# Attention with the keys on the partitions: maxima from a rough pass, no transposed weights

## What is computed

```
s = einsum('bkgqd,bskd->bkgqs', q, k) * scale
p = softmax(s, axis=-1)
o = einsum('bkgqs,bskd->bkgqd', p, v)
```

## Time and profile before

| | us |
|---|---|
| median of 3 runs | 1509.86 (1509.58 to 1510.22) |
| the profiled execution | 1512.08 |
| its span, first to last instruction | 1510.1 |
| TensorE busy | 1382.5 (92%) |
| VectorE busy | 920.6 (61%) |
| ScalarE busy | 597.4 (40%) |
| GpSimd busy | 519.5 (34%) |

### The profile page before, as it was taken

The page is one execution under the profiler, slowest core; times in us unless marked ns, Lnnn a source line. Parts: engine busy times, 40 slices in busy tenths (PEclk is TensorE's granted clock), DMA queues, the critical chain, the costliest instruction groups (busy, mean ns, idle before and its releaser), DMA issues.

```text
span 1510.1 us, 14992 instructions
## 1 busy us (share of the span) xinstructions
PE 1382.5 (92%) x5743; PEld 1029.7 (68%) x5743; DVE 920.6 (61%) x981; ACT 597.4 (40%) x931; POOL 519.5 (34%) x239
## 2 busy tenths in 40 slices
PE   5999888888999999999979997787979999999997
PEld 3677655455788888878746774554758888887885
DVE  4766875545687787711176777664467787884112
ACT  4422355543544434422242225564344344333222
POOL 2322311014444444354452213100353444444444
PEclk8999897989999999999989999898989999999997
DMA  7212310002233333323341222000213333323332
GB/s 241 85 29 63 77 33 12 1 29 84 64 90 98 98 91 91 94 88 93 88 139 45 68 56 71 15 1 0 71 56 98 88 94 98 97 87 88 98 94 66
DMA packets 205472, 112.49 MB, mean 74 GB/s; under 512 B 15239, under 2 KB 202361, under 8 KB 204506
## 3 DMA queue, kind: packets, MB, share of 16 engines
q1 hardware_dynamic: 205402, 111.54, 25.5%
HBM read 105.63 MB, written 2.10 MB: 71 GB/s over the span
## 4 chain that ended last, share of the span: by engine, by line
PE 75%; DVE 12%; ACT 6%; issue 3%; POOL 2%; DMA 1%; SPq 1%; DVEq 0%; POOLq 0%; ACTq 0%
PE ps L938 19%; PE ps L940 19%; PE ps L939 19%; PE ps L1217 3%; PE ps L1032 2%; PE ps L1006 2%; PE ps L1193 2%; PE ps L1089 1%; ACT prob L739 1%; DVE p L1432 1%; POOL xT L468 1%; ACT wh L520 1%; PE ps L948 1%; PE ps L1045 1%; DVE tb L1344 1%
## 5 line engine op out<-in xcount | busy, mean ns | idle before, releaser
L461 POOL TENSOR_TENSOR wl<-raw,wh 128x1024 fp32r<-128x1024 f32 x184 | 447.9, 2436 | 868.0 <-ACT wh L520 867.9
L520 ACT ACTIVATE wh<-raw 128x1024 fp32r<-128x1024 f32 x184 | 195.0, 1060 | 599.3 <-PE ps L940 559.5
L938 PE MATMUL ps<-gh,wh 128*128 128x512 f32 (+1 forms) x896 | 364.2, 406 | 6.6 <-POOL wl L461 6.6
L940 PE MATMUL ps<-gh,wl 128*128 128x512 f32 (+1 forms) x896 | 355.8, 397 | 0.0
L939 PE MATMUL ps<-gl,wh 128*128 128x512 f32 (+1 forms) x896 | 355.7, 397 | 0.0
L938 PEld LDWEIGHTS ps<-gh,wh 128*128 128x128 f32 (+1 forms) x896 | 167.9, 187 | 54.2 <-issue 11.4
L939 PEld LDWEIGHTS ps<-gl,wh 128*128 128x128 f32 (+1 forms) x896 | 167.6, 187 | 45.8 <-issue 5.4
L940 PEld LDWEIGHTS ps<-gh,wl 128*128 128x128 f32 (+1 forms) x896 | 167.6, 187 | 42.5 <-issue 0.8
L1741 DVE SCALAR_TENSOR_TENSOR cv<-pad,pm,cv 128x512 f32<-128x512 f32 x88 | 130.5, 1483 | 84.4 <-ACT cv L840 84.4
L1328 DVE TENSOR_TENSOR acc<-acc,sq 128x512 f32<-128x512 f32 x24 | 60.6, 2524 | 195.7 <-ACT sq L564 195.5
L938 PE MATMUL ps<-fh,wh 128*128 128x512 f32 x352 | 139.4, 396 | 3.2 <-POOL wl L461 3.2
(11 more groups left out here) (228 smaller groups left out, 1900.9 us busy)
## 6 DMA issues: line engine op xcount, KB each, us to landing
raw<-w_up SPq DMA_DIRECT2D x88, 512.0 KB, 3.8
raw<-w_down SPq DMA_DIRECT2D x32, 512.0 KB, 4.1
raw<-w_in SPq DMA_DIRECT2D x30, 512.0 KB, 3.9
raw<-w_out SPq DMA_DIRECT2D x16, 512.0 KB, 4.3
raw<-w_down SPq DMA_DIRECT2D x16, 384.0 KB, 3.5
xio<-x SPq DMA_DIRECT2D x4, 512.0 KB, 4.4
win<-c_win SPq DMA_DIRECT2D x2, 1024.0 KB, 4.9
TF<-c_tf SPq DMA_DIRECT2D x2, 1024.0 KB, 8.9
```

The lines of the kernel that those rows point to most:

```text
L461: nc.gpsimd.tensor_tensor(wl[:, slot, :], raw[:, slot, :], wh[:, slot, :].bitcast(F32), ALU.subtract).then_inc(S["lo_ready"], 1)
L520: A(wh[:, slot, :], raw[:, slot, :], ACT.Copy).then_inc(S["hi_ready"], 1)
L938: mm(ps[0:cols, bank, :], w_hi, x_hi, start=start and k == 0, stop=False)
L940: ins = mm(ps[0:cols, bank, :], w_lo, x_hi, start=False, stop=stop and k == tile_n - 1)
```

## The change

Score tiles are now computed with the keys on the partitions, so their exponentials are at once the operand that `values` needs, and nothing is transposed. The maximum of a query is then along partitions no longer reachable by a bias; it is added by TensorE:
- `peaks` (PE) makes a rough pass: one fp32r matmul a tile (query high and low half against the keys' high half only; for MLA fp32r copies of keys and queries that ACT makes in `mla_hi`), with queries on the partitions, in banks 0 and 1. `maxima` reads these tiles.
- `shift` (POOL) multiplies ident by the four negated maxima of each partition: a 128x512 diagonal diag, two buffers.
- `scores` (PE) computes a tile with two matmuls (one fp32 matmul for MLA) and adds a third, the product of a matrix of ones and diag, which puts the negated maximum of its query on every element. Three banks (2 to 4) rotate.
- `exp` (ACT) has no bias and no accumulator and writes probT, of which there are now four.
- `row_sums` (DVE) adds key tiles 0 and 1 to 2 and 3 of a head, and `denominators` (PE) sums over partitions by a product with ones, in bank 7, whose order of use is now written out in B7_ORDER. `inverse` (ACT) takes a logarithm and an exponential.
- `values` alternates between banks 5 and 6 and is spread over the tiles of the next head. Queries have three buffers (Q2) instead of two.
- The rough tiles of head 0 stand around and inside item 15, `klo` behind the first maxima, group work is placed one to three heads later, and two of POOL's output-item low halves have shift 0 between them.
- The matrix of ones is made by POOL as fp32r in the prologue.

The diff, cut to its core; the bodies of `turn`, `pt_copy`, `inv_wide`, `inv_copy`, `inverses` and the old loops, which are removed, are left out.

```diff
-        prob = sb("prob", [P, 2, TC, T])
+        tsum = sb("tsum", [P, 2, 2, T])
+        probT3 = sb("probT3", [P, TC, T])
...
+            diag = sb("diag", [P, 2, T], F32R, s)
+            q2c = sb("q2c", [P, T], F32R, s)
+        probT = [probT0[:], probT1[:], uc[:, 2:6, :], probT3[:]]
+        Q2 = [q2[:, 0, :], q2[:, 1, :], q2c[:]]
+        KMLA = [ka[:, 0, :], kb[:, 0, :], ka[:, 1, :], kb[:, 1, :]]
...
-        B7_FIRST = {0: 0, 1: 1, 3: 3}
-        B7_SECOND = {1: 2, 3: 4, 5: 5, 6: 6, 7: 8}
-        B7_FIRST[7] = 7
-        B7_STAT = 5
+        B7_FIRST = {1: 0, 2: 2, 4: 3, 7: 6, 8: 7}
+        B7_SECOND = {1: 1, 4: 4, 6: 5, 8: 8}
+        B7_ORDER = [("item", 0), ("item", 1), ("item", 2), ("den", 0), ("item", 3), ("item", 4), ("den", 1), ("group", 0),
+                    ("item", 5), ("item", 6), ("den", 2), ("item", 7), ("item", 8), ("den", 3), ("group", 1), ("den", 4),
+                    ("den", 5), ("group", 2)]
         HEADS = GH + MH
         PAIRS = HEADS // 2
+        N_TILES = HEADS * TC
+        S_BANK = lambda h, sc: 2 + (h * TC + sc) % 3
+        N_BANK = lambda h, qc: (h * TC + qc) % 2
+        assert N_TILES % 3 == 0 and N_TILES % 2 == 0
...
+                def shift(h):
+                    pool.wait_ge(S["nmax"], lay * N_TILES + (h + 1) * TC)
+                    if h >= 2:
+                        pool.wait_ge(S["s_tile"], lay * N_TILES + (h - 1) * TC)
+                    nc.gpsimd.tensor_tensor(diag[:, h % 2, :].rearrange("p (c n) -> p c n", c=TC),
+                                            ident[:].unsqueeze(1).to_broadcast([P, TC, P]),
+                                            nm[:, h % 2, :].unsqueeze(2).to_broadcast([P, TC, P]),
+                                            ALU.mult).then_inc(S["shift"], 1)
...
-                for slot in range(2):
-                    lo(lay * ITEMS + (I_OUT + slot), slot)
+                lo(lay * ITEMS + I_OUT, 0)
+                shift(0)
+                lo(lay * ITEMS + I_OUT + 1, 1)
                 pool.wait_ge(S["lo_ready"], lay * ITEMS + I_OUT + 4)
-                for h in range(2, GH):
-                    q_lo(h)
-                    pool.wait_ge(S["q2lo"], lay * GH + h + 1)
+                for h in range(1, HEADS):
+                    shift(h)
+                    if h + 1 < GH:
+                        pool.wait_ge(S["shift"], lay * HEADS + h + 1)
+                        q_lo(h + 1)
+                        pool.wait_ge(S["q2lo"], lay * GH + h + 2)
...
+                def mla_hi(i):
+                    h = GH + i
+                    if i == 0:
+                        act.wait_ge(S["mk_in"], (lay + 1) * 16 * MH)
+                        act.wait_ge(S["mq_in"], (lay + 1) * 16 * 2 * MH)
+                    act.wait_ge(S["b7_free"], lay * len(B7) + 4 + i // 2)
+                    act.wait_ge(S["s_tile"], lay * N_TILES + TC * max(4 + 4 * (i // 2), h - 2))
+                    A(KMLA[i][0:MD, :], mkf[0:MD, i, :], ACT.Copy).then_inc(S["m_hi"], 1)
+                    A(Q2[h % 3][0:MD, :], mqf[0:MD, i, :], ACT.Copy).then_inc(S["m_hi"], 1)
+                def exp(h, sc):
+                    act.wait_ge(S["s_tile"], lay * N_TILES + h * TC + sc + 1)
+                    if h >= 4 and sc == 0:
+                        act.wait_ge(S["pv"], lay * PAIRS + (h - 4) // 2 + 1)
+                        act.wait_ge(S["summed"], lay * HEADS + h - 3)
+                    A(probT[h % 4][:, sc, :], ps[:, S_BANK(h, sc), :], ACT.Exp).then_inc(S["p_ready"], 1)
+                def inverse(p):
+                    act.wait_ge(S["den_mm"], lay * PAIRS + p + 1)
                     if p >= 2:
                         act.wait_ge(S["y_pair"], lay * PAIRS + p - 1)
+                    inverse_root(rr[:, p % 2, :], std[:], ps[:, 7, :], 1, bias=False).then_inc(S["den_inv"], 1)
+                    act.wait_ge(S["den_inv"], lay * PAIRS + p + 1)
...
+                    exp(h, 0)
+                    if h == 0:
+                        hi(lay, I_OUT + 1, 1)
                     if h + 2 < GH:
                         q_hi(h + 2)
+                    exp(h, 1)
+                    exp(h, 2)
                     if h == 0:
                         root(6, MKVR)
+                    if h == HEADS - 1:
+                        group_root(1)
+                    exp(h, 3)
+                    if h >= 3 and h % 2:
+                        inverse((h - 3) // 2)
...
+                        if t == WIN - 1 and k in (2, 3):
+                            peaks(0, [k])
...
+                def peaks(h, tiles_):
+                    for qc in tiles_:
                         cols = slice(qc * P, (qc + 1) * P)
+                        i = h * TC + qc
+                        if i < 2:
+                            pe.wait_ge(S["evac"], lay * WIN + WIN - 2)
                         else:
+                            pe.wait_ge(S["nmax"], lay * N_TILES + i - 1)
+                        if qc == 0 and h < GH:
+                            pe.wait_ge(S["q2hi"], lay * GH + h + 1)
+                            pe.wait_ge(S["q2lo"], lay * GH + h + 1)
+                            if h == 0:
+                                pe.wait_ge(S["khi"], lay * 4 + 4)
+                        if qc == 0 and h >= GH:
+                            pe.wait_ge(S["m_hi"], lay * 2 * MH + 2 * (h - GH) + 2)
                         if h < GH:
+                            q, k = Q2[h % 3][:, cols], ka[:, h // 4, :]
                         else:
+                            q, k = Q2[h % 3][0:MD, cols], KMLA[h - GH][0:MD, :]
+                        mm(ps[:, N_BANK(h, qc), :], q, k, start=True, stop=True).then_inc(S["n_tile"], 1)
+                def scores(h, sc):
+                    i = h * TC + sc
+                    bank = S_BANK(h, sc)
+                    if i >= 3:
+                        pe.wait_ge(S["p_ready"], lay * N_TILES + i - 2)
+                    elif i == 0:
+                        pe.wait_ge(S["nstd"], lay * 7 + 6)
+                        pe.wait_ge(S["klo"], lay * 4 + 4)
+                    elif i == 1:
+                        pe.wait_ge(S["vcopy"], lay + 1)
+                    else:
+                        pe.wait_ge(S["evac"], lay * WIN + WIN - 1)
+                    keys = slice(sc * P, (sc + 1) * P)
+                    if h < GH:
+                        mm(ps[:, bank, :], ka[:, h // 4, keys], Q2[h % 3], start=True, stop=False)
+                        mm(ps[:, bank, :], kb[:, h // 4, keys], Q2[h % 3], start=False, stop=False)
+                    else:
+                        mm(ps[:, bank, :], mkf[0:MD, h - GH, keys], mqf[0:MD, h - GH, :], start=True, stop=False)
+                    if sc == 0:
+                        pe.wait_ge(S["shift"], lay * HEADS + h + 1)
+                    mm(ps[:, bank, :], ones_r[:], diag[:, h % 2, :], start=False, stop=True).then_inc(S["s_tile"], 1)
...
+                def values(p, tiles_):
+                    bank = 5 + p % 2
+                    if 0 in tiles_:
+                        if p == 0:
+                            pe.wait_ge(S["evac"], lay * WIN + WIN)
+                        elif p == 1:
+                            pe.wait_ge(S["nstd"], lay * 7 + 7)
+                        else:
+                            pe.wait_ge(S["y_pair"], lay * PAIRS + p - 1)
+                        if p == GH // 2:
+                            pe.wait_ge(S["b7_free"], lay * len(B7) + len(B7))
+                        pe.wait_ge(S["p_ready"], lay * N_TILES + (2 * p + 2) * TC)
                     for sc in tiles_:
                         for half in range(2):
                             h = 2 * p + half
                             v = vg[:, sc, (h // 4) * GD:(h // 4 + 1) * GD] if h < GH else mv[:, sc, (h - GH) * MV:(h - GH + 1) * MV]
+                            ins = mm(ps[half * GD:(half + 1) * GD, bank, :], v, probT[h % 4][:, sc, :], start=(sc == 0),
                                      stop=(sc == TC - 1))
+                    if TC - 1 in tiles_:
+                        ins.then_inc(S["pv"], 1)
+                def denominators(p):
+                    free7("den", p)
+                    pe.wait_ge(S["summed"], lay * HEADS + 2 * p + 2)
+                    for part in range(2):
+                        for half in range(2):
+                            ins = mm(ps[half * GD:(half + 1) * GD, 7, :], ones[:, 0:GD], tsum[:, half, part, :],
+                                     start=(part == 0), stop=(part == 1))
+                    ins.then_inc(S["den_mm"], 1)
                 for h in range(HEADS):
+                    after = h + 1 < HEADS
+                    p = (h - 2) // 2
+                    whole = h >= 2 and h % 2 == 0
+                    rest = h >= 3 and h % 2
+                    scores(h, 0)
+                    if after:
+                        peaks(h + 1, [0, 1])
+                    scores(h, 1)
+                    if h in B7_FIRST:
                         bank7(B7_FIRST[h])
+                    if h == 6:
```

(48 more changed lines are left out.)

230 lines of the change are left out of this document (56 added, 174 removed).

## The result

| | before | after |
|---|---|---|
| median, us | 1509.97 (4 runs) | 1498.18 (1497.40 to 1500.31, 4 runs) |
| the profiled execution (its span) | 1512.08 (1510.1) | 1497.4 (1495.4) |
| mean granted clock | 0.954 | 0.977 |

The ratio is 0.9924, with a 95% interval of 0.9907 to 0.9942: 11.8 us faster, where 32 were forecast. The measured time lies 1.2 us above the range.

A forecast was written before the change was run, and what follows sets the result against it. TensorE bounds the kernel, with 36.2 of 119.45 us a layer idle or at half clock. 187.1 + 91.1 + 5.2 + 6.5 + 3.3 + 5.5 = 298.7 against 314.85, 16.2 us a layer; forecast 1477.5 us, range 1450 to 1497.

The forecast's parts named there:

- Start: Layer start: first exact score tile at 187.1 us, then 5.2 us of waiting for shift 1 and query 2's low half.
- TensorE's work: From the first exact tile on: rough tiles, scores, values, denominators and bank-7 products at full-clock pitches, 91.1 us a layer.
- one pair of heads' values 3.58: Value products on TensorE: start-to-start pitch of 3.58 us a pair, 21.5 a layer; denominators taken as half, 1.8.
- Loop waits: Head loop: TensorE waits 6.5 us a layer for late VectorE, at head 3 and behind head 8's group squares.
- Shift: POOL's ident times broadcast maxima: 1.3 to 1.6 us, covered by 2.7 to 3.5 us when VectorE is on time.
- Row sums: VectorE's sums of key tiles, twelve a layer: 1.15 to 2.4 us each, any of which may meet a POOL instruction.
- Clock: Attention stage: two idles a layer that lower the granted clock, about 2.7 us each, 5.5 together.
- Tail: End of stage: output item's low halves 2.1 us late and last statistics 1.2 us late, 3.3 together.
- the second: Rival: VectorE becomes the bound through the port lock, 9 us a layer less gain, 1495.5 us; chance 0.17.
- The fourth: Rival: waits only change names, 36.2 us a layer lost as now, no change, 1509 us; chance 0.06.
- The third: Rival: POOL's shift is slow, gain gone at 4.35 us, 1537.5 us at a shift of 5.5; chance 0.07.
- The first: Rival: TensorE is the only bound, only the start wait stays, 31.5 us a layer gained, 1447 us; chance 0.15.

The follow-up runs named there:

- e12: The changed kernel with only GpSimd's low half of output item 17 moved behind the query's low half of head 2: 1494.44 us, ratio 0.9887.
- e2: The changed kernel with VectorE's row sums of heads 2, 4, 6 and 8 one head later, behind the denominators they wait for: 1499.41 us, ratio 0.9932.
- e7: The changed kernel without VectorE's row sums, denominators made from key tiles 0 and 1 only: 1499.38 us, ratio 0.9919.
- e4: The changed kernel with ACT's two conversions for an MLA head ahead of the inverse in odd heads: 1496.99 us, ratio 0.9923.
- e10: e4 with the two group sums and MLA items 5 and 6 (bank 7) in another order: 1488.85 us, ratio 0.9855.
- e8: The changed kernel with GpSimd making each diagonal twice, one behind the other: 1512.59 us, ratio 1.002.
- e1: The changed kernel with three value slices of even heads together where the first stood, the fourth of odd heads directly before the denominators: 1510.19 us, ratio 1.000.
- e6: As e1, but the three value slices stand behind rough tiles 2 and 3 instead of ahead of them: 1514.49 us, ratio 1.0027.
- e11: e10 with e12's edit, GpSimd's low half of item 17 behind the query's low half of head 2: 1482.41 us, ratio 0.9814.
- e13: e11 with the fourth value slice of each pair behind the last score tile, directly ahead of the denominators: 1479.98 us, ratio 0.9809.

## Why the prediction was right or wrong

By its own steps, for the first layer, the sum's value first:
- **Start**: first exact tile at 187.1, measured 186.09 (item 15 ended at 185.0, forecast 185.5; VectorE's low half took 3.56 where 4.2 was taken). The waits behind it 5.2, measured 5.0, for shift 1 and query 2 as named. Right. e12 took 1.65 of them away with one line's place.
- **TensorE's work**: 91.1. By distances it was 90.6, so the counts were right, but the groups of column halves cost 8.8 more. **This is the largest mis-sized term, and the first step that failed.** The step "one pair of heads' values 3.58" took the price from a block of four slices, where one group's cost is spread over the four and partly outside the number, and used it for four slices placed one by one, and "half of 3.58" for the denominators. The 3.58 holds 0.14 of it. Against 91.1, work and groups came to 99.4: 8.3 us a layer were missed. The change's line "spread over the tiles of the next head" was read and not priced. The Trainium skill has a sentence for it (TensorEngine Tiling (Array Packing), Key Properties): changing the tiling mode drains TensorE. It gives no price. The trace has a loss of 0.35 us for going there and back, which fits; that it is a drain, no row shows.
- **Loop waits**: 6.5, measured 10.7 and 2.4 hidden in pairs of rough tiles. This is the second step that failed, in place and in size. The mechanism named, row sums that wait for denominators at head 3, cost next to nothing (e2), and VectorE's whole row-sum load is 1.2 us, some 3 at equal clock (e7). The waits stood where the prediction wrote "free": MLA's conversions queued on ACT behind the inverse (2.7; e4), and group work (1.31, 1.95, 1.01) that the change had placed later and whose new places were never set against TensorE's order (e10). The sign given, the largest waits in heads 1 to 5 on maxima and shift, held for the 2.35 us alone.
- **Shift**: taken at 1.3 to 1.6, measured 1.04 in the median, below the lower end (1.41 and 1.63 for heads 0 and 1). Hidden from head 2 on, as forecast, and with the cover given: in e8 3.22 us were hidden too. Not in the prediction: the query half behind it has less cover (e8).
- **Row sums**: 1.15 to 2.4, measured 1.22 in the median and 2.08 at most. On the lock the prediction cited the Trainium skill (SBUF — State Buffer, SBUF: two separate sides); the rows agree with it (3.43 us behind a GpSimd instruction, 1.22 alone), and it decides little here.
- **Clock**: 5.5, measured 1.6. The forecast had two falls a layer at 2.7; one came, behind the wait of 2.35. (The timeline of the kernel before has three idles of 2 us and more, 4.05, 2.49 and 2.03, and one of 1.97, not four or five, so its 13 us make over 3 each.) This error, 3.9 us, went the other way and hid a part of the first two. It was luck as far as the working goes: e1, e6 and e8, with waits of the same kind, lose 5 to 12 us to the clock in layer 0.
- **Tail**: 3.3; two waits of 1.38 and 0.87 us, of which 1.0 shows from out to w_up (59.5 after 58.5). Over-sized by 2.3 as it stands, but some 1.7 of that is again the clock. The kernel before:
```profile
320.00:340.00 20.00, 17.59 (x69) 13.82 (x68) 9.02 (x7) 8.54 (x13) 6.68 (x3) 0.91 0.18 53
```
The changed kernel has 1.00 in this stretch (shown at e4). At equal clock the tail is 2.7 longer, near the forecast.

Summed: work and groups +8.3, loop waits +6.6, small steps +1.8, start waits -0.2, clock -3.9, first tile -1.0, tail -2.3: 9.3 us a layer less gain than 16.2, which is the 6.9 measured.

Of the rivals, the second named 1495.5 us, near the measured time, for a reason that e7 and e2 refute: it wanted 9 us a layer from VectorE and the lock, and no more than 3 are there. The fourth (waits only change names) is closer than its chance said: TensorE lost 36.2 us of 119.45 before, and loses 30.3 of 120.9. It is wrong in the names and about the clock, since 8.8 of the 30.3 are no wait at all and half clock fell from about 13 to 1.6 us. The third didn't occur, and even e8's doubled shift shows little of it: only head 1's diagonal is late. The first (TensorE the only bound) would need no waits and no groups.

That e11 and e13, with the same work in another order, run at 1482.4 and 1480.0 us (28 and 29 less than the kernel before) with a stretch of 111.8 in e11 against the 108 to 112 forecast says what the change comes to when its helpers' queues are set to it. That this is near 1477.5 is partly two errors of opposite sign, since the groups are still in it. What the kernel before would gain from the same care with its queues was not tried, so not all of the 28 us need be the change's.

## What to carry to other kernels

Price a matmul from a row that has the same neighbours: one that is split out of a block of its kind is dearer than its share of the block, here by 0.35 us each time TensorE goes from full width to column halves and back. Where a change moves small work "a few heads later" on three queues, walk every moved instruction against the engine that waits for it, the ones off the bound engine first: here such places cost 7 us a layer (1.35 twice, 1.31, 1.95 and 1.01), and putting them right, with the one at the start, took 16 us off the kernel. And a filler that costs something can still be right where it stands, as long as it covers a wait. Read the granted clock beside every difference between two stages before naming its cause: in e1, e6 and e8 half or more of it was the clock.

## What had not been expected of the hardware

- 64-column matmuls side by side cost 0.35 us a group beyond their own 0.86 a slice at 2.4 GHz (0.09 ahead, 0.15 inside, 0.11 behind), though no wait is recorded. A change from fp32 to fp32r at full width costs nothing: an MLA tile with its diagonal product takes 1.09 us (294.14, 295.23, 296.32), which is 0.86 + 0.23.
- GpSimd's product of two broadcast inputs, 128x512, takes 1.04 us alone, less than its subtraction of 64x512 without a broadcast, 1.27.
- The same pause does not always bring the clock down. At item 18 the engine stood 2.41 us in the kernel before and ran at 1.2 GHz half a microsecond later (steps of 0.43 us from 330.10 on), 2.34 us in the changed kernel and stayed at 2.4, 2.35 us in e4 and fell. So a gain of 2 to 3 us in the stage can be given back by half in the next one. What decides it wasn't tried.
